# Seven products instead of eight in more projection panels of a two-layer decoder trunk, and weight quarters combined in place

## What is computed

```
proj = h @ w_in          # 2048 x 5392: q, k, v | DeltaNet q, k, v, z | a, b
attn = sliding_window_attention(rope(q), rope(k), v, sinks)
o    = gated_delta_rule(l2norm(dq), l2norm(dk), dv, g, beta)   # chunked, with a triangular solve
o    = o * rsqrt(mean(o*o) + eps) * dn_norm_w * silu(z)
mix  = concat([attn, o]) @ w_out                               # 2048 x 2048
x    = layer_norm(ALPHA * x + mix)
x    = layer_norm(ALPHA * x + grouped_moe(x))                  # 16 experts, top 2 in one group
```

## Time and profile before

| | us |
|---|---|
| median of three runs (1997.31 to 1998.77) | 1997.37 |
| the profiled execution | 1998.46 |
| its span, first to last instruction | 1996.7 |
| PE busy / DVE / ACT / POOL | 1921.4 / 686.5 / 329.5 / 103.0 |
| mixer of layer 0, to the end of panel 14 | 508.3 |
| experts of layer 0, first gate matmul to last pair | 533.7 to 984 |
| panel 14 of layer 1 ends | 1494.7 |

### The profile page before, as it was taken

How to read it: one execution, slowest core, us unless ns; L and a number is a source line. 1 busy time by engine, 2 the same in 40 slices (tenths; PEclk the granted TensorE clock), 3 DMA queues, 4 the chain that set the end, 5 groups by cost and what they waited for, 6 DMA issues and landing times.

```text
span 1996.7 us, 27957 instructions
## 1 busy us (share of the span) xinstructions
PE 1921.4 (96%) x11409; PEld 1194.3 (60%) x11409; DVE 686.5 (34%) x1385; ACT 329.5 (17%) x616; POOL 103.0 (5%) x174
## 2 busy tenths in 40 slices
PE   8999999999999999999899999999999999999996
PEld 7888886666644434444488888766665444443443
DVE  5444434553501111111483434445534011111104
ACT  1104220110311110111211231111103111110112
POOL 4000030012000000000000001200210000000000
PEclk9999999999999999999999999999999999999998
DMA  7433342228699999999934434422397999999995
GB/s 243 148 127 127 127 148 86 85 64 321 271 408 422 422 422 422 422 422 422 406 112 146 139 112 147 135 75 68 103 368 275 411 421 422 422 422 422 422 421 243
DMA packets 128842, 539.16 MB, mean 270 GB/s; under 512 B 15856, under 2 KB 20464, under 8 KB 78320
## 3 DMA queue, kind: packets, MB, share of 16 engines
q1 hardware_dynamic: 128752, 537.86, 69.0%
HBM read 535.73 MB, written 2.10 MB: 269 GB/s over the span
## 4 chain that ended last, share of the span: by engine, by line
PE 68%; DMA 25%; DVE 5%; issue 1%; ACT 0%; SPq 0%; DVEq 0%; ACTq 0%
PE bank L860 17%; DMA ring<-in_w_down_dram 13%; DMA ring<-in_w_up_dram 12%; PE bank L1405 10%; PE bank L871 9%; PE bank L919 8%; PE bank L1453 6%; PE bank L1190 3%; PE bank L953 3%; PE bank L1337 3%; PE bank L787 1%; DMA x_t<-in_w_up_dram 1%; PE bank L1066 1%; PE bank L1349 0%; PE bank L1161 0%
## 5 line engine op out<-in xcount | busy, mean ns | idle before, releaser
L860 PE MATMUL bank<-x_t,ring 128*128 128x256 f32 x1536 | 342.6, 382 | 0.0
L860 PEld LDWEIGHTS bank<-x_t,ring 128*128 128x128 f32 x1536 | 288.4, 190 | 48.8 <-issue 11.2
L2333 DVE TENSOR_TENSOR region_a<-bank,region_a 128x512 f32<-128x512 f32 x16 | 11.1, 692 | 566.3 <-PE bank L1405 566.3
L1405 PE MATMUL bank<-ring,region_a 128*64 128x512 f32 x704 | 159.6, 596 | 13.1 <-DMA ring<-in_w_up_dram 13.1
L1337 PEld LDWEIGHTS bank<-prob_t,x_nat 128*128 128x128 f32 x1024 | 115.5, 192 | 12.0 <-issue 11.4
L871 PE MATMUL bank<-ring,mix_acc 128*128 128x512 f32 x256 | 121.3, 604 | 1.4 <-ACT mix_acc L1663 1.4
L1453 PE MATMUL bank<-ring,region_a 128*64 128x512 f32 x512 | 115.1, 594 | 5.9 <-DMA ring<-in_w_down_dram 5.8
L1337 PE MATMUL bank<-prob_t,x_nat 128*128 128x128 f32 x1024 | 118.6, 277 | 0.0
L1405 PEld LDWEIGHTS bank<-ring,region_a 128*64 128x64 f32 x704 | 51.6, 137 | 109.3 <-issue 107.6
L1453 PE MATMUL bank<-region_b,region_a 128*64 128x512 f32 x384 | 113.3, 596 | 1.7 <-ACT region_a L1710 1.7
L2346 DVE SCALAR_TENSOR_TENSOR y_lo<-bank,slot_gate,y_hi 128x512 fp32r<-128x512 f32 x64 | 48.0, 750 | 193.1 <-ACT y_hi L1722 187.9
(11 more groups left out here) (424 smaller groups left out, 2413.0 us busy)
## 6 DMA issues: line engine op xcount, KB each, us to landing
ring<-in_w_up_dram SPq DMA_DIRECT2D x88, 1024.0 KB, 19.5
ring<-in_w_in_dram SPq DMA_DIRECT2D x80, 1024.0 KB, 5.0
ring<-in_w_down_dram SPq DMA_DIRECT2D x64, 1024.0 KB, 23.4
region_b<-in_w_gate_dram SPq DMA_DIRECT2D x48, 1024.0 KB, 19.6
region_b<-in_w_down_dram SPq DMA_DIRECT2D x48, 1024.0 KB, 20.6
ring<-in_w_gate_dram SPq DMA_DIRECT2D x36, 1024.0 KB, 22.4
ring<-in_w_out_dram SPq DMA_DIRECT2D x32, 1024.0 KB, 5.2
x_t<-in_w_up_dram SPq DMA_DIRECT2D x32, 1024.0 KB, 19.1
```

What stands on the lines that cost most here:

```text
L860: m = pe.matmul(b[c // 2][:, (c % 2) * T:(c % 2 + 1) * T], w[:, kk, c * P:(c + 1) * P], xT[:, k, :], start=(k == 0 and c % 2 == 0), stop=( ...
L1405: m = pe.matmul(bank[2 + w][rows, :], xg_half[k // 8][:, k % 8 * P + rows.start:k % 8 * P + rows.stop], weights(n + e)[:, kk * PANEL:(kk + ...
```

## The change

It has four parts.
1. FAST now has panels 1, 2, 9 and 10 whole (28 units each), the front half of the contraction of panels 11 to 14 (pieces j = 0, 1, which need only the attention heads; 14 units each) and the back half (j = 2, 3) of panels 11 to 13. Only the back half of panel 14 stays plain: 16 steps. Each half is collected and added to `x_nat` by itself (`add_half`).
2. `combine` writes into the quarters themselves. So it can't start when the piece has landed, but when PE has done P1, and its third instruction when PE has done P3 (`raw_done`). The products P1, P2, P3 of a piece come first, then those of the next piece, and only then P5, P7, P6, P4 of the first (`units_of`).
3. `left` holds the units of panel 10, of the four front halves and the first seven of panel 11's back half: 91 units. The DVE work for them stands at fixed places of the DeltaNet part (`between`).
4. Panel 8 is computed 256 columns after 256 columns, the banks are dealt anew, and SP issues expert pieces 0 to 3, 12 and 13 together behind the last piece of panel 14.

```
-    FAST = [1, 2, 9, 13]
+    FAST = [(1, (0, 1, 2, 3)), (2, (0, 1, 2, 3)), (9, (0, 1, 2, 3)), (10, (0, 1, 2, 3))]
+    FAST += [(i, (0, 1)) for i in range(N_IN, N_IN + 4)]
+    FAST += [(i, (2, 3)) for i in range(N_IN, N_IN + 3)]
+    GATE0, GATE1, FRONT, BACK = 2, 3, 4, 8
...
-                if m >= 2:
-                    pool.wait_ge(combined_free.sem, combined_free.at(l, m - 1))
-                pool.tensor_tensor(t1, b12, b11, ALU.subtract).then_inc(combined_ready.sem, 1)
+                pool.wait_ge(raw_done.sem, raw_done.at(l, 2 * m + 1))
+                pool.tensor_tensor(b11, b12, b11, ALU.subtract).then_inc(combined_ready.sem, 1)
...
             for l in range(depth):
-                for f in range(2, N_FAST):
-                    for j in range(4):
+                for f in range(GATE0, N_FAST):
+                    for j in FAST[f][1]:
                         combine(l, f, j)
...
+                def units_of(f):
+                    pieces = FAST[f][1]
+                    loaded = [[(f, j, name) for name in AS_LOADED] for j in pieces]
+                    mixed = [[(f, j, name) for name in COMBINED] for j in pieces]
+                    if f == BACK:
+                        return loaded[0] + mixed[0] + loaded[1] + mixed[1]
+                    units = loaded[0]
+                    for n in range(1, len(pieces)):
+                        units = units + loaded[n] + mixed[n - 1]
+                    return units + mixed[-1]
...
-                left = [(10, k, t) for k in range(KC) for t in range(NT)]
-                left += [(i, k, t) for i in (11, 12) for k in range(8) for t in range(NT)]
-                left += [(i, k, t) for i in (11, 12) for k in range(8, 12) for t in range(NT)]
+                left = [unit for f in range(GATE1, BACK) for unit in units_of(f)] + units_of(BACK)[:7]
...
-                            meanwhile(len(left))
-                            for i, k in last_quarters[:-1]:
-                                k_step(i, k, (0,))
+                            meanwhile(len(left) - 2)
...
-                fast_panel(13)
+                meanwhile(len(left))
+                fast_panel(BACK, 7)
+                fast_panel(BACK + 1)
+                fast_panel(BACK + 2)
                 last_panel()
...
-                        for k in range(KC):
+                        for k in range(KC // 2, KC):
...
-                combine(1, 0)
                 for i in range(2):
...
-                        for j in range(1, 4):
+                        for j in range(4):
                             combine(1, j)
...
+                def between(half, lev):
+                    if (half, lev) == (0, 2):
+                        dve.wait_ge(pv_read.sem, pv_read.at(l, n_q // 2))
+                        add_sums(mixT, front_sums, 0, 4)
+                    if (half, lev) == (0, 4):
+                        collect_second_sixth(GATE1)
+                        collect_fifth_seventh(GATE1)
+                    if (half, lev) == (0, 5):
+                        collect_third_fourth(GATE1)
+                    if (half, lev) == (1, 1):
+                        collect_third_fourth(FRONT + 1)
+                    if (half, lev) == (1, 2):
+                        add_half(FRONT + 1)
+                    if (half, lev) == (1, 4):
+                        add_sums(mixT, back_sums, 4, 6, 4)
...
                         dve.wait_ge(o1_done.sem, o1_done.at(l, 1))
+                        collect(FRONT)
+                        add_half(FRONT)
...
                         m.then_inc(masked_ready.sem, 1)
+                        between(half, lev)
                         dve.wait_ge(tlt_done.sem, tlt_done.at(l, n_tlt + lev))
```

More of the change, by code:

```diff
@@ L913, in fast_unit @@
-                    if name in ("P6", "P5", "P7", "P4"):
-                        seen = {"P6": 2, "P5": 2, "P7": 3, "P4": 4}[name]
-                        pe.wait_ge(combined_ready.sem, combined_ready.at(l, 4 * m + seen))
-                    _, at, half = next(x for x in PRODUCTS if x[0] == name)
-                    o = bank[FAST_BANKS[i][at]][:, half * HW:(half + 1) * HW]
+                        if i >= N_IN and j < 2:
+                            pe.wait_ge(pv_read.sem, pv_read.at(l, n_q // 2))
+                        elif i >= N_IN:
+                            pe.wait_ge(to_read.sem, to_read.at(l, j))
@@ L918, in fast_unit @@
+                    if name == "P3":
+                        pe.wait_ge(sums_ready.sem, sums_ready.at(l, 1 + j // 2 if i < N_IN else 3 if j < 2 else 2 + j))
+                    if name in COMBINED:
+                        pe.wait_ge(combined_ready.sem, combined_ready.at(l, 4 * m + 1 + COMBINED.index(name)))
+                    at, half = PRODUCTS[name]
+                    o = bank[FAST_BANKS[f][at]][:, half * HW:(half + 1) * HW]
                     for a in range(2):
[L919 to L920 removed]
+                        mm = pe.matmul(o, lhs[:, a, :], rhs[:, a, :],
+                                       start=(j == pieces[0] and a == 0 and name in FIRST_IN_BANK),
+                                       stop=(j == pieces[-1] and a == 1), skip_group_check=True)
@@ L1101, in _ @@
                     .then_inc(gc_done.sem, 1)
-                panel(8)
+                for side in range(2):
+                    for k in range(KC):
+                        k_step(8, k, (side,))
                 pe.wait_ge(rows_ready.sem, rows_ready.at(l, 1))
@@ L1665, in _ @@
                             .then_inc(to_read.sem, 1)
-                copy_first(3)
+                for f in range(BACK, N_FAST):
+                    copy_first(f)
                 for t in range(NT):
@@ L1794, in add_sums, with blocks_of @@
                     s.do(tt(s3, a11, a21, ALU.subtract))
                     s.sync()
+                    s.link(tt(s2, s1, a11, ALU.subtract))
                     tt(s4, a12, s2, ALU.subtract).then_inc(sums_ready.sem, 1)
-                def collect(f, to, start, row):
-                    _, b, c, d = (bank[n] for n in FAST_BANKS[FAST[f]])
+                def blocks_of(to, start, row):
                     outer = to[:, start:start + 2 * (row + HW)].rearrange("p (a n) -> p a n", a=2)[:, :, 0:HW]
@@ L1817, in collect, with add_half @@
                     dve.wait_ge(fast_read.sem, fast_read.at(l, 3 * f + 3))
+                def collect(f):
+                    collect_second_sixth(f)
+                    collect_fifth_seventh(f)
+                    collect_third_fourth(f)
+                def add_half(f):
+                    i = FAST[f][0] - N_IN
+                    xs = x_nat[:, :, i * PANEL:(i + 1) * PANEL]
+                    held, at = half_panel(f)
+                    mixed = held[:, at:at + NT * PANEL].rearrange("p (t n) -> p t n", t=NT)
+                    if f < BACK:
+                        s.do(stt(out=xs, in0=xs, scalar=ALPHA, in1=mixed, op0=ALU.mult, op1=ALU.add))
+                    else:
+                        s.do(tt(xs, xs, mixed, ALU.add))
@@ L1892, in _ @@
                 dve.sem_inc(roped.sem, 1)
-                combine(0, 3)
+                for j in range(1, 4):
+                    combine(0, j)
                 if l:
@@ L2121, in _ @@
                     m.then_inc(inv_ready.sem, 1)
+                    if half:
+                        collect(FRONT + 2)
+                        add_half(FRONT + 2)
                     if half == 0:
```

357 lines of the change are left out of this document (166 added, 191 removed).

## The result

| | before | changed |
|---|---|---|
| median, us (five runs each) | 1997.37 | 2008.07 |
| lowest to highest | 1997.07 to 2000.46 | 2007.40 to 2009.32 |
| span of the profiled execution | 1996.7 | 2006.3 |

The changed kernel takes 1.0048 times as long (95% interval 1.0037 to 1.0059): 10.7 us slower, where 9.2 us faster was forecast. The time lies outside the range.

The account below looks back on a forecast made before the run. PE was taken to bound the mixer and the weight stream the expert stage. Gains of 12.9 us per layer less losses left 6.35; twice that less 3.5 is 9.2 us, giving 1988 us, range 1980 to 1999.

Parts of the forecast that it names:

- 1, products, and the wait behind the turn: Behind the DeltaNet part: fewer products gain 11.9 us per layer, covering PE's wait behind the last turn gains 0.7.
- 1, panel 9's small waits: Panel 9: PE's small waits for POOL shrink by some 0.3 us per layer.
- 2, the LayerNorm behind the end: End of the mixer: tile 1's LayerNorm on DVE starts some 1.35 us later after PE's end, per layer.
- 4, instructions added on DVE: DeltaNet part: sums overrun DVE's gap by 0.5 us, instructions ahead of the decay matrices cost 0.7, panel 12's collect 0.6.
- 4 and 5, meetings with POOL: DeltaNet part: DVE delayed beside POOL, 1.0 us at level 0, 1.0 at the head norm, one meeting at the second half's start.
- 6, POOL as a pace: Panel 11's back half: POOL's differences come later than PE's P4 needs them, 0.7 us (0.3 to 1.5) for two pieces.
- 6, panel 3: Panel 3 needs collect's first instruction right behind panel 2's P4: 0.2 us lost per layer.
- 3, start of layer 1, once: Panel 2 of layer 1: PE waits for DVE 1.4, 0.3 and 2.4 us; 3.5 us lost once (2.5 to 4.5).
- Elsewhere the pieces fall into DVE's gaps: DeltaNet part: apart from the meetings listed, POOL's pieces cost nothing, with PE's fillers set on the old times.
- The rival "Slower": DVE's two-SBUF-input instructions on the path meet POOL 15 times per layer at 0.96 us: 2009 us, chance 0.08.
- The sign named for it: DVE's L2070, L2086 and L2090 would take near 1.7 us if the slower rival held.
- The two tests for the whole prediction: Wrong if the DeltaNet part grows under 2 or over 8 us, or the stretch to the panels' end isn't near 57.5.

Follow-up runs that it names:

- e1: Changed kernel with all of POOL's 112 combining instructions per layer on 4 of 512 columns, so part of the computation is left out: 2041.46 us.
- e4: Changed kernel with POOL doing the same work but held at four places until DVE is past its two-SBUF-input instructions on the path: 1996.56 us.
- e3: Changed kernel with the six pieces of the back halves combined by DVE instead of POOL, nothing left out: 1997.52 us.
- e2: Changed kernel with only the six back-half pieces combined on 4 of 512 columns, so part of the computation is left out: 1997.53 us.
- e6: Changed kernel with DVE's addition of panel 11's front half moved from ahead of the second half's decay matrices to behind L2120: 2007.74 us.
- e5: Changed kernel with layer 1's two multiplications of x_nat by the gain moved into DVE's two earlier gaps: 2004.84 us.
- e7: Changed kernel with the edits of e3, e4, e5 and e6 together: 1978.43 us, ratio 0.9893 to the kernel before.
- e8: e7 without one of POOL's four holds: panel 14's first piece no longer waits for the head norm of tile 0: 1982.34 us.
- e9: The same kernel as e7, run again: 1978.30 us, ratio 0.9901 to the kernel before.

## Why the prediction was wrong, step by step

What bounds the kernel, where the fillers stop saving anything, and that the mixer's time passes to the expert stage one for one were right: layer 0's first expert gate matmul moved by 1.54 us (535.18 for 533.64), layer 1 began 1.51 later (998.15 for 996.64). Per layer, in us:

| step of the prediction | foretold | measured | from |
|---|---|---|---|
| 1, products, and the wait behind the turn | +12.6 | +12.9 | e1: 70.69 - 57.78 |
| 1, panel 9's small waits | +0.3 | +0.05 | 26.73 for 26.78 us |
| 2, the LayerNorm behind the end | -1.35 | -1.1 | 26.63 for 25.53 to the experts |
| 4, instructions added on DVE | -1.8 | -1.5 | e1: 141.17 - 139.71 |
| 4 and 5, meetings with POOL | -2.5 | -6.6 | 147.76 - 141.17 |
| 6, POOL as a pace | -0.7 | -6.2 | 63.94 - 57.78 |
| 6, panel 3 | -0.2 | -0.2 | 1.09 for 0.86 us from panel 2's last unit |
| 3, start of layer 1, once | -3.5 | -5.05 | 74.32 - 69.27 |

In layer 0 PE also reached panel 9 0.8 us earlier (270.12 for 270.93, panel 3's 0.2 included), which was not forecast: the first half of its kv panel took 1 us less (3.46 for 4.45). The runs differ there: the DeltaNet part begins between 296.68 and 298.12. With it the rows of layer 0 sum to -1.6, against 1.54 measured; layer 1 lacks it and loses 2.6 behind its start. Together with that start it makes 9.1 us at the first expert matmul of layer 1 (1529.20 for 1520.09), and 0.5 more came in its expert stage. Of the range: the high bounds of the prediction's terms sum to 11.05 us, not 11.5, and the low ones to 3.05 with panel 3; that moves its ends by under 1 us.

**Step 6 failed first, by 5.5 us per layer.** "A piece costs POOL 5.1 us and PE 6.04, so POOL keeps up where pieces are interleaved" compares two rates, and rates decide only where the follower can work ahead. A back half has two pieces, and POOL may touch the first only after its P1. From the end of that unit to P4 of the second piece PE has 12 units, 10.4 us; POOL has eight differences. Their step is 1.34 us, not 1.27: 0.08 us lies between two of them (starts at 474.96, 476.30, 477.64). With 0.36 us to start, that is 0.36 + 7 x 1.34 + 1.27 = 11.0 us, 0.6 late; one meeting with L1851 on top (L628 for 2.13 instead of 1.27) makes it 1.5. It is the measured loss of panels 12 and 13, for which the prediction had put nothing. In panel 11, where it had put 0.35 for each piece, it had set P4 against the end of the differences with 5.1 us; start and four differences are 0.35 + 3 x 1.34 + 1.27 = 5.6, and P4 is due after 4.3, so 1.3 for the second piece, and one meeting more for the first. The prediction had in its own rows that POOL's second instruction takes 1.60 beside DVE and used 5.1 all the same.

**The meetings (steps 4 and 5) had the right price and the wrong count.** The price came from the earlier trace rows: 1.07 us for L2140, and the same instruction is now stretched by 0.95. The places taken were level 0 of the first half (two), the start of the second half (one) and the head norm ("three times instead of once", against slack of 0.1, yet set at 1.0). Eight met POOL on the path (one had done so before): two, one, two at level 0 of the second half, where none had been counted, and three. Their costs to PE were 1.45, 0.8 (1.44 less the 0.65 that e4 left), 2.1 (2.31 less the 0.22 of e4) and 1.5, together 5.9 of the 6.6. "Elsewhere the pieces fall into DVE's gaps" rested on fillers at their old times; but P1 of panel 13 is the second of three fillers ahead of level 0, so POOL starts (396.79) just ahead of L2146 (396.87). The sequence of units was known, and this one could have been read from it. Two in a row both meet: POOL's next instruction starts 0.08 us after its last, ahead of DVE's.

The Trainium skill ("SBUF — State Buffer", Who interferes with whom) has the two as excluding each other for a whole instruction. The trace agrees: L1851 begins at 469.31 and takes 1.86 us, while POOL's L626 ends at 470.10; L628 begins at 470.18 and takes 2.13. Each waits for the other in turn: L1851 ends 1.07 after L626, and L628 ends 1.14 after L1851.

**Step 3 was right in its waits** (0.96 and 2.19 us where 1.4, 0.3 and 2.4 were put) and left out what followed them, the 1.7 us of low clock. Without it the loss is 3.4.

**The rival "Slower" gave 2009 us, and 2008 was measured, but it is only half of what happened.** It was made of fifteen meetings per layer; there are eight on the path, 6.6 us. The other half, the pace, it did not have. That its time was met is luck. The sign named for it, L2070, L2086 and L2090 near 1.7 us, showed in part: L2119 (L2070) took 1.46 once, one mask of the first half (L2086) 1.4 instead of 0.4, L2090's successor kept its time. The two tests for the whole prediction both came out against it, the first narrowly: the DeltaNet part grew by 8.05, over 8, and the last stretch took 63.5 behind the turn, not 57.5. The range left this rival out at 0.08, too little for a mechanism of which every single meeting had been priced at a full microsecond while slacks of 0.1 to 1.1 us were all that stood against it.

## What to carry to other kernels

When a helper engine prepares operands in place, compare not its rate with the consumer's but the time from the event that lets it begin to the first use of its last result, with the gap between instructions counted; a run in which it hardly works gives the bound at once. Here an instruction of VectorE with two SBUF inputs and one of GpSimd ran one behind the other, at 0.7 to 1.1 us a meeting, so list those on the critical path and see from the order of the units what GpSimd does at each. Work with slack can then be held back by a wait until the other engine is past its tight place: four such waits, one exchange of engine and two changes of VectorE's order turned 0.5% slower into 1% faster with all the work still in it.

## What the runs showed of the hardware

Not expected was the **fall of TensorE's clock behind a single short wait**, in some executions and not in others. It fell to the 1.2 GHz level for about 3.5 us, in these profiled executions:

| PE's wait | low clock behind it | full clock behind it |
|---|---|---|
| 2.19 us, start of layer 1 | changed, e1, e3, e4 | e2, e6 |
| 2.31 us, level 0 of the second half, layer 0 | e5, e6 | changed, e2, e3 |
| the same in layer 1 | e3, e6 | changed, e2, e5 |
| 0.96 or 0.97 us with one of 0.3 to 0.6 ahead of it, expert stage of layer 1 | changed, e3, e5, e6 | before, e2, e4, e7, e8, e9 |

The last row, first the changed kernel, then the one before:

```profile
1559.46 5.77 PE L1448 MATMUL bank<-region_b,region_a 128*64 128x512 f32 x17 [0.97 <-ACT region_a L1707]
...
1550.71 4.07 PE L1453 MATMUL bank<-region_b,region_a 128*64 128x512 f32 x17 [0.96 <-ACT region_a L1710]
```

So the length of the wait alone does not decide. It cost 1.7 us where PE is the bound. With the long waits removed (e7, e9) it is gone from the mixers, so removing a wait of 2.2 us can give back almost twice its length. Runs of one kernel differ by it too: e2's ten fall into four of 1993.73 to 1994.84 at a mean granted clock of 0.997 or 0.998, and six of 1997.03 to 1999.69 at 0.994 or 0.995; the profiled one, with no fall, is of the first group. The medians of kernels that have such waits carry a share of this.

What stays open: why it follows a wait in one execution and not in another was not tried.
